# Seventeen early U products instead of fourteen in a one-core decoder layer: two in each middle routing step, and the loads of their U blocks issued by ACT

## What is computed

```
q = (xb @ w_query).reshape(tb, PEER_HEADS, 2, PEER_HALF)
s = jnp.einsum('thpc,hpnc->thpn', q, sub_keys, ...)
top_s, top_i = lax.top_k(s, PEER_TOPK)
...
best_s, best_pos = lax.top_k(cand_s, PEER_TOPK)
idx = jnp.take_along_axis(cand_i, best_pos, axis=-1)
g = jax.nn.softmax(best_s, axis=-1)
u = expert_u[idx]
h = jax.nn.gelu(jnp.einsum('thkd,td->thk', u, xb, ...), approximate=False)
w = (g * h).astype(xb.dtype)
return jnp.einsum('thk,thkd->td', w, expert_v[idx])
```

## Time and profile before

| what | value |
| --- | --- |
| median of the three runs | 2706.05 us |
| the profiled execution, its own time | 2707.24 us |
| its span, first to last instruction | 2705.4 us |
| mean granted TensorE clock | 0.985 of full speed |
| PE busy | 2560.8 us (95%) |
| DVE busy | 2242.5 us (83%) |
| POOL busy | 1301.4 us (48%) |
| ACT busy | 906.4 us (34%) |
| the three busiest parts of the chain that ended last | PE h_psum L1763 21%, PE o_psum L2246 15%, PE g_psum L2246 9% |

### The profile page before, as it was taken

One profiled execution on the slowest core, in us unless ns is written; L12 is line 12 of the kernel. 1 busy time (PEld: TensorE's weight loads), 2 busy tenths in 40 slices (PEclk: granted clock), 3 DMA queues, 4 the chain that ended last, 5 costly groups with the idle time before them and its releaser, 6 DMA issues.

```text
span 2705.4 us, 45691 instructions
## 1 busy us (share of the span) xinstructions
PE 2560.8 (95%) x16973; PEld 1682.1 (62%) x17163; DVE 2242.5 (83%) x4525; ACT 906.4 (34%) x1602; POOL 1301.4 (48%) x864
## 2 busy tenths in 40 slices
PE   8999979999978878999999999999999999999996
PEld 5777646689977755665565565565565664664652
DVE  2444456668899987799998998999999999998998
ACT  2433335511135545532232232232332332331324
POOL 2200010100044441276777766777666676766772
PEclk9999979999999998999999999999999999999998
DMA  6000213320024466899999999999999999999995
GB/s 228 29 17 17 86 63 121 135 81 27 27 63 131 122 212 198 329 405 394 372 380 377 363 382 366 364 376 380 351 384 365 361 383 377 363 388 351 358 338 221
DMA packets 282028, 695.55 MB, mean 257 GB/s; under 512 B 30680, under 2 KB 113112, under 8 KB 275552
## 3 DMA queue, kind: packets, MB, share of 16 engines
q0 software_dynamic: 110592, 402.70, 39.2%
q1 hardware_dynamic: 170224, 287.84, 29.9%
q10 hardware_dynamic: 1008, 2.29, 0.3%
HBM read 631.51 MB, written 61.24 MB: 256 GB/s over the span
## 4 chain that ended last, share of the span: by engine, by line
PE 52%; issue 9%; DVE 7%; DMA 6%; POOL 4%; ACT 1%; SPq 0%; POOLq 0%; ACTq 0%; DVEq 0%
PE h_psum L1763 21%; PE o_psum L2246 15%; PE g_psum L2246 9%; PE r_t_psum L1218 4%; DMA early<-u_rows,pick_index 3%; POOL rt_hot L1455 3%; PE h_psum L1268 2%; POOL early L1770 1%; DMA rt_u_pre<-u_blocks 1%; DVE rt_hot L1662 1%; DVE early L2087 1%; DMA early<-u_blocks 1%; PE r_s_psum L1230 1%; DVE rt_hot L1672 1%; DVE rt_top_u L1507 0%
## 5 line engine op out<-in xcount | busy, mean ns | idle before, releaser
L1763 PE MATMUL h_psum<-early 128*128 128x384 bf16 x5448 | 759.0, 299 | 0.4 <-ACT act_out L1957 0.4
L1763 PEld LDWEIGHTS h_psum<-early 128*128 128x128 bf16 x5448 | 532.6, 98 | 224.3 <-issue 0.9
L1770 POOL DMA_INDIRECT early<-u_rows,pick_index x320 | 460.8, 1440 | 205.3 <-DVE dots L2087 115.8
L1770 POOL DMA_INDIRECT early<-v_blocks,pick_index x320 | 454.0, 1419 | 199.3 <-DVE wide L2091 118.7
L2246 PE MATMUL o_psum<-v_split,w_split 128*128 128x512 bf16 x2293 | 538.0, 379 | 1.4
L2091 DVE SCALAR_TENSOR_TENSOR wide<-early,dots,wide 128x1024 f32<-128x1024 f32 x320 | 405.4, 1281 | 24.5 <-DMA early<-v_blocks,pick_index 23.6
L2087 DVE CUSTOM_DVE_ANT_0 early<-early,wide 128x1024 f32<-128x1024 f32 x320 | 387.8, 1221 | 37.3 <-DMA early<-u_rows,pick_index 33.2
L2246 PEld LDWEIGHTS o_psum<-v_split,w_split 128*128 128x128 bf16 x2304 | 225.5, 98 | 271.8
L2246 PE MATMUL g_psum<-v_split,w_split 128*128 128x512 bf16 x1400 | 343.4, 379 | 14.5 <-DVE wide L2079 4.6
L1965 ACT ACTIVATE v_split<-early 128x512 bf16<-128x512 f32 x256 | 159.4, 624 | 326.5 <-PE o_psum L2246 303.3
L2246 PEld LDWEIGHTS g_psum<-v_split,w_split 128*128 128x128 bf16 x1536 | 149.9, 98 | 172.6 <-issue 8.7
(11 more groups left out here) (239 smaller groups left out, 3278.3 us busy)
## 6 DMA issues: line engine op xcount, KB each, us to landing
early<-v_blocks SPq DMA_DIRECT2D x256, 256.0 KB
early<-u_blocks SPq DMA_DIRECT2D x114, 512.0 KB
gates<-wide SPq DMA_DIRECT2D x16, 2048.0 KB, 9.2
gate<-gates SPq DMA_DIRECT2D x32, 1024.0 KB
early<-w_query SPq DMA_DIRECT2D x8, 1024.0 KB, 5.6
gates_late<-wide SPq DMA_DIRECT2D x4, 2048.0 KB, 6.9
gate<-gates_late SPq DMA_DIRECT2D x32, 256.0 KB
rt_u_pre<-u_blocks SPq DMA_DIRECT2D x14, 512.0 KB, 4.7
```

What stands on the lines that cost most here:

```text
L1763: mm = pe.matmul(bank(half)[:, 0:width * P], u_split[:, k, part, c], xs[:, first:first + width, xpart, c, :], start=(c == 0 and part == 0 ...
L1770: pool.indirect_dma_start(row, None, source, bass.IndirectOffsetOnAxis(ap=pick_index[:, tile, at:at + 1], axis=0)).then_inc(arrived, 16)
```

## The change

- The early products become 17. `PRE_PIECES` says how many pieces follow each slot of each step: in the middle steps none in slots 0 to 3, then 1, 1, 1, 2, 2, 2, 2, 3, 4, 4, 5, 5, which is 32 pieces or two products; step 4 has 5 in each slot, and 8 (`PRE_TURNED`) behind the picks' turn instead of ten ahead of it; step 5 has 3 in each of the slots 0 to 7. `PRE_BLOCKS` is 6, 13, 20, ..., 118, so 111 blocks instead of 114 have their U product in the expert phase.
- PE and ACT have the middle steps written out (`for` instead of `Fori`).
- From product 4 on ACT stores h itself, and behind that issues the load of the U block of the product after next into the buffer that has just come free. SP loads the first six only.

```
-PRE_AHEAD, PRE_STEPS, PRE_LAST = 4, DENSE - 2, 7
-PRE = PRE_AHEAD + PRE_STEPS + PRE_LAST
-PRE_BLOCKS = tuple(6 + 9 * k for k in range(PRE))
+PRE_AHEAD = 4
+PRE_PIECES = ((0,) * 4 + (1,) * 3 + (2,) * 4 + (3,) * 1 + (4,) * 2 + (5,) * 2,) * (DENSE - 2) + (
+    (5,) * 16, (3,) * 8 + (0,) * KD)
+PRE_TURNED = (0,) * (DENSE - 2) + (8, 0)
+PRE = PRE_AHEAD + (sum(map(sum, PRE_PIECES)) + sum(PRE_TURNED)) // PIECES
+PRE_BLOCKS = tuple(6 + 7 * k for k in range(PRE))
...
-        STEP_PIECES = {8: 1, 9: 1, 10: 2, 11: 2, 12: 3, 13: 3, 14: 4}
-        STEP_COPIES = {13: 0, 15: 1}
-        FIRST_PIECES = 10
-        LAST_PIECES = {DENSE - 2: (5,) * SLOTS, DENSE - 1: (3,) * (U_FIRST - 2) + (2,) * 2 + (0,) * KD}
-        PRE_LOADS = {12: 8, 13: 9, 14: 10, 15: 11}
+        PRE_COPIES = pre_copies()
...
                 def step(d):
                     s = d + GATHERED
-                    made = 0
                     turn_picks(d - 1, 4 * s + 3)
...
                         gate_batch(d - 1, m)
-                        if m in STEP_PIECES:
-                            pre(d + (PRE_AHEAD - 1), made, made + STEP_PIECES[m])
-                            made += STEP_PIECES[m]
+                        pieces(PRE_PIECES[d - 1][m])
 
                 def last_steps(d):
-                    made = PIECES * (PRE_AHEAD + PRE_STEPS)
                     if d < DENSE - 1:
-                        for piece in range(made, made + FIRST_PIECES):
-                            pre(piece // PIECES, piece % PIECES, piece % PIECES + 1)
                         turn_picks(d, 4 * TILES)
+                    pieces(PRE_TURNED[d])
...
-                with pe.Fori(1, DENSE - 1) as d:
+                for d in range(1, DENSE - 1):
                     step(d)
...
-                    if half == 1 and isinstance(k, int) and k >= PRE_AHEAD + PRE_STEPS:
+                    if half == 1 and k >= PRE_AHEAD:
                         act.wait_ge(h_copied, 2 * (k + 1))
                         act.dma_start(h_early[k], h_out[:, :]).then_inc(pre_stored, 16)
+                        if k + 2 < PRE:
+                            act.dma_start(u_pre[:, k % 2], u_blocks[PRE_BLOCKS[k + 2]]).then_inc(pre_in[k % 2], 16)
```

77 lines of the change are left out of this document (28 added, 49 removed).

## The result

| | before | after |
| --- | --- | --- |
| median of the runs | 2706.05 us (5 runs, 2704.59 to 2710.22) | 2688.84 us (5 runs, 2681.17 to 2691.85) |
| ratio to before | | 0.9925, 95% interval 0.9908 to 0.9942 |
| the profiled execution, its own time | 2707.24 us | 2683.10 us |
| its span | 2705.4 us | 2681.3 us |
| PE busy | 2560.8 us (95%) | 2565.9 us (96%) |

The change makes the kernel 17.2 us faster by the medians, about half of the 36.4 forecast, and the median lies outside the range. The ratio compares the means of the runs, and by it the gain is 20 us; two of the five runs lie inside the range.

A forecast was written before the change was run, and what follows sets the result against it. PE's matmul stream was taken to bound the expert phase and DVE the middle routing steps. From 2706.05 us, -19.6 + 1.4 - 5.6 - 12.6 = -36.4 gave 2669.6 us, range 2662 to 2684.

The forecast's parts named there:

- Part A: Expert phase: three U products of 6.52 us leave PE's stream, DVE's work fitting into the shorter time; -19.6 us.
- second rival: The expert phase stops being PE's alone; half of Part A turns into PE waiting for DVE: 2679.5 us, chance 0.10.
- Part D: Steps 4 and 5: with ACT issuing U-block loads, PE's two load waits and half clock behind them go; -12.6 us.
- rival 4: ACT's queue: load issues block for 7.8 us, so gates aren't copied and DVE waits; +37.8, 2743.9 us, chance 0.03.
- what is late next?: Step 5: DVE, PE and ACT nearly equal per slot, at least 38 us; 1 us left for the close race.
- closing sentence: Step 5: wrong as a whole if PE's waits move from loads to ACT, which copies gates 1.98 of 2.4 us.
- rule that I weighed against part D: All issuers' DMAs share 16 engines, a second issuer saves only issue time; most of Part D lost, 2680 us.
- Part B: Middle steps: three more early products hide behind DVE; later turns of picks cost 0.7 us at two boundaries, +1.4 us.
- Part C: Boundary from step 3 to 4: five small pieces instead of ten ahead of the picks' turn, DVE starts earlier; -5.6 us.

The follow-up runs named there:

- fetch_first: The changed kernel with POOL's five gathers of rows issued ahead of POOL's part of step 5 instead of behind it: 2679.55 us.
- taken_17: The kernel before, routing still making 14 early products but the expert phase taking 17 blocks as made, three U products left out: 2695.44 us.
- after again: The changed kernel unchanged, run and profiled a second time: 2686.31 us.
- thin_v: The changed kernel without the loads of every second half V block in the expert phase: 2680.58 us.
- act_loads: The kernel before, with ACT instead of SP issuing the last five loads of U blocks: 2698.91 us.
- turn_first: The changed kernel with the five pieces behind slot 15 of each middle step moved behind the turn of the picks that follows: 2680.25 us.
- taken_17_clear: As taken_17, with blocks 35 and 96 in place of 34 and 97: 2688.20 us.
- clear_blocks: The changed kernel with early blocks 35 and 96 in place of 34 and 97: 2682.02 us.

## Why the prediction was wrong, by its parts

**Part A failed, and it is the largest miss.** Forecast 19.6, measured 10.4 alone. Three products are worth that much of PE's stream. Take the stretch from the second U product to the last V product and subtract PE's waits and half of its busy time at the lower granted clock (an estimate, from PE's timelines and the clock): before leaves 1566.6 us, and after, fetch_first and taken_17 leave 1547.7, 1547.5 and 1547.4, 19 us less. What took the gain back is what was subtracted: 8.6 us of waits and no lower clock in before, 10.4 + 4.6 in the first profile of after, 12.7 + 1.9 in taken_17, 15.0 + 4.1 in fetch_first. The step that failed is "DVE's work fits into the shorter time: it has 115 us free". DVE's idle time isn't room: 66 of the 115 us were waits for gathered rows, in a view (DVE's own waits) that I didn't open. The second fault stands beside it: rows 3 show three waits of PE for the sums, and I read their total, 4.6 us, as proof that nothing happens. They were 0.87 us at 1457 (block 33), 2.56 at 2499 (block 114) and 1.21 at the end of the last first half. Each sits where a U product is missing, and the change decides anew where those places are. That was to be had from PE's order and the list of blocks. The second fault decides the price: with the same work for DVE and two blocks moved, part A alone gives 18 to 19 us. DVE late costs PE little where a U product stands in between.

This was the second rival, with its price nearly right (half of part A) and its chance, 0.10, too low. What spoke for it in the text, DVE at 93% and DMA at 0.98, I had set aside with "PE hardly ever waits for what DMA brings". True of PE, not of DVE, and DVE stands between them. The Trainium skill (Perfetto Trace Analysis, Identifying the Most-Contended Engine) warns that the occupancy of 16 DMA engines misleads and asks for HBM utilization, the bytes moved against the memory's rate. Here both moved together: from 1112 to 2660 us share 0.98 at 371 GB/s in after again, 0.95 at 350 in thin_v, and the waits for rows fell from 87 to 49 us.

**Part D: mechanism right, half of its size lost.** The loads land after a median of 7.9 us, where I took 9.9, and no product waits for one. ACT's issue isn't 0.35 us but 0.57 to 1.40, median 1.16: that much of rival 4 was there, far below its 4.4. What the last load gained is first its place in the order: SP sent it at 1060.85, right behind a store of gates that it sent at 1060.28, and ACT in act_loads sent it at 1049.95. Issuing from ACT alone was worth 7.0 us of 12.6. What I asked and didn't answer was "what is late next?": I compared engines and left out the stage buffers. The closing sentence named the place, "PE's waits move from loads to ACT", but not its cause, a store of 17.4 us beside POOL's five gathers. They stood at 1052 to 1058 us in the trace of before, and I had not looked at POOL's queue there, nor at where the store would fall once its gates came 6 us sooner. Where they are moved away, step 5 gives 14.0 us. On the rule that I weighed against part D, the Trainium skill (DMA: Bandwidth & Descriptors, Issuing engines are not separate DMA queues): its half on issue time fits the rest of the gain, 6.45 of the last load's 12.28 us being SP's issue, against 0.46 of 3.8 in act_loads. Its other half, that all issuers' transfers interleave on the same engines, was borne out by a transfer that I hadn't asked about, 9.1 against 17.4 us.

**Part B: 2.5 us and not 1.4.** Steps 1 and 2 take 72.29 and 72.42 us from first to first key one-hots, 71.11 and 71.10 before: 1.2 and 1.3 us. The turn came at 909.04 in the profiled run of after, and the step before it had begun 2.7 us late (838.03 against 835.35, of which 1.5 stem from an earlier phase): the slots' own part was right, no DVE wait in slots 5 to 9. Missed are 0.5 to 0.6 us per boundary: the turn comes some 0.4 us later behind the start of its step than I had it, and DVE's start a little later behind the turn. In the trace PE waits 0.2 to 0.4 us for ACT's copies in slot 14, where ACT copies and stores h and issues a load; no run tests that part by itself. turn_first shows that the whole price was avoidable.

**Part C was nearly right, with some luck:** step 3 takes 72.47 us and not 77.42, 5.0 us less against 5.6. But the 7.93 us of the ten pieces, from which I took it, stand at a granted clock of 0.78. In taken_17, with the same routing program, they run at 1.00:

```profile
976.03 6.24 PE L1269 MATMUL h_psum<-x_t,rt_u_pre 128*128 128x384 f32 x20
```

There and in taken_17_clear step 3 takes 75.7 us, and against these two part C is 3.2 us. Which of the two is the rule for before isn't shown; act_loads has 77.4.

**The sum.** 10.4 + 7.0 + 5.0 - 2.5 = 19.9 us from parts measured alone or at one place; the changed kernel gave 17.2 in its first five runs and 20.2 in the next group (2706.55 - 2686.31). Of the 36.4 forecast, 9.2 are missing in A, 5.6 in D, 1.1 in B and 0.6 in C. The edits of fetch_first, turn_first and clear_blocks bring 35.9 us by undoing these misses. That this meets the forecast so closely is in part chance: B costs nothing any more where 1.4 us were allowed for, and step 5 gives 14.0 us where 12.6 were.

## What to carry to other kernels

An engine's idle time counts as room only after its own waits are read: DVE's 115 us held 66 us of waiting for DMA. Where a schedule leaves work out at every seventh place, look at which of these places coincide with a handover between engines (two of 17 here cost 4 to 9 us), and price a handover by what covers it. When a wait is removed, look for what the earlier work now meets, on every queue: the store that had come behind the gathers came among them, and half of the gain went into it.
